# Loading and transposing x ahead of the adaLN product, with the small loads on ScalarE's queue

## The chip, the cores and the metric

The kernel runs on one core of a Trainium2 chip. The metric is the device time of one execution in microseconds; the kernel before takes 868.68 us (median of three executions).

## The reference

One layer of a decoder: 512 tokens, width 1024, float32. Only its beginning matters here:

```python
c_act = silu(c)
mod = c_act @ ada_w + ada_b                 # 1024 -> 6 * 1024
shift1, scale1, gate1, shift2, scale2, gate2 = split(mod, 6)
u = x * (1.0 + scale1) + shift1
q, k, v, lru_x, lru_gate, gate_a, gate_b = split(u @ w_in)   # 1024 -> 5376
y = sigmoid(gate_a) * attention(q, k, v) + sigmoid(gate_b) * rg_lru(lru_x) * gelu(lru_gate)
x = layer_norm(ALPHA * x + gate1 * (y @ w_out))
# then a routed mixture of 16 experts, and a second layer norm
```

So nothing of the large product `u @ w_in` can start before the first third of `mod` (shift1 and scale1, "mod1") is there, which needs 8 MB of `ada_w`, and before x is there.

## The kernel before

Each engine has an instruction stream written out by hand; semaphores order them. Products are taken channel-major: u is held transposed (`uT`, 8 blocks k of 128 channels by 512 tokens), and each weight tile and u are split into a rounded float32r part and the rest (`uh`, `ul`; `whi`, `wlo`), so that a product is three matmuls (L1267 to L1269).

SyncE (SP) issues, in this order: the constants (`cst`, L372, 346 KB, with the identity for transposes), `ccol`, four broadcast pieces of `ada_b` (L375), five small parameter loads (L383), eight 1 MB slices of `ada_w` (`ada1`, L385), four 512 KB pieces of x (L387), and the first three weight tiles of `w_in` (L395; tiles 0, 1, 2, each 512 KB in runs of 512 bytes). Then it stores a small bias table (L405), waits for that store, loads two 512 KB weights of the recurrence (`wax`, L423 and L424) and goes on with the weight tiles from tile 3. Weight tile t waits until the buffer of tile t-3 is split (`split_lo`). Between tiles 5 to 8 it also issues four replications of the bias table, DRAM to DRAM, 768 KB each (L411), and after tile 6 two small copies of k (L433, L434).

GpSimd (POOL) issues at the start twelve small loads, the last of them `rbr` (L511); from the first finished block of `ul` on it loads sixteen further 1 MB slices of `ada_w` (`ada2`, L518) through three buffers, which TensorE frees.

TensorE (PE) works in this order: transpose of the parameters (L1225), the bias table (L1228, which waits for all twelve loads of POOL), the product with `ada1` (`modulate`, L1233, eight steps j, each waiting for its slice), the transpose of its result (L1243), then the 32 transposes of x (L1253) into four PSUM banks, then `project(0)`, `project(1)` and so on, one for each weight tile; the products with `ada2` and the work of the attention and of the recurrence stand between them.

VectorE (DVE) adds the bias (L841), writes shift and scale (L844, L845), then for each pair of blocks computes the odd block of u out of PSUM (L860) and the low parts of both (L856). After the first pair it splits weight tile 0, after the last pair tile 1 (L832); then comes a chain of 24 tiny operations (L870 to L885), and then the split of tile 2. ScalarE (ACT) computes for an even block `uh` and `uT` out of PSUM (L610, L611), for an odd block `uh` out of `uT` (L607), and the high parts of the weight tiles (L589).

Because PE's four banks are refilled only when ACT and DVE have read them, the transposes of the blocks 4 to 7 wait for the blocks 0 to 3.

Of the kernel before, what the change touches and what calls it, by code (L numbers as in the profile page):

```python
# [9 lines left out]
ACT = mybir.ActivationFunctionType  # L10
# [6 lines left out]
P = 128  # L17
D = 1024
KT = D // P
T = 512  # L20
NT = T // P
# [48 lines left out]
C_ID, C_LOW, C_HOT, C_TOK, C_EXP, C_LT, C_GT, C_END = 0, 128, 256, 640, 644, 660, 676, 692  # L70
# [32 lines left out]
def hybrid_layer(nc, x, c, ada_w, ada_b, w_in, attn_sink, rel_bias, conv_w, conv_b, lru_wa, lru_ba,  # L103
# [13 lines left out]
    with ctx:  # L117
# [10 lines left out]
        def at(offset, name, shape, dt=F32):  # L128
            size = 4 * int(np.prod(shape[1:]))
            assert offset + size <= 229344, name  # L130
            return nc.alloc_sbuf_tensor_at(name, shape, dt, offset=offset), offset + size
# [45 lines left out]
        x_sb, _ = at(R_A, "x_sb", [P, NT, D])  # L177
        uT, _ = at(R_B, "uT", [P, KT, T])
        uh, _ = at(R_U, "uh", [P, KT, T], F32R)
# [144 lines left out]
        def sem(name):  # L324
# [16 lines left out]

        names = """setup_done pcol_ps bvec_ps xT_ps u_even u_odd mod1_ps mod1_sb u_hi u_lo split_hi split_lo proj_ps evac
            pcol_sb exp_small dve_order pool_order c_done bvec_sb k_sb conv_done lr_ps li_ps er_done ti_done
# [27 lines left out]
        def _(sp):  # L371
            sp.dma_start(cst[:, :], consts[:, 0:C_END]).then_inc(const_in, 16)  # L372
            sp.dma_start(ccol[:, :], c[0].rearrange("(p j) -> p j", j=8)).then_inc(small_in, 16)
            for g in range(4):
                sp.dma_start(adab1[32 * g:32 * g + 32, :], ada_b[0, g * 512:(g + 1) * 512].partition_broadcast(32))\  # L375
                    .then_inc(adab_in, 16)
            for j, (a, b) in enumerate(((conv_w[0].rearrange("j (k p) -> (j k) p", p=P), 32),
                                        (conv_b[0].rearrange("(k p) -> k p", p=P), 8),
                                        (lru_ba[0].rearrange("(k p) -> k p", p=P), 8),
                                        (lru_bx[0].rearrange("(k p) -> k p", p=P), 8),  # L380
                                        (lru_lambda[0].rearrange("(k p) -> k p", p=P), 8))):
                r = (0, 32, 40, 48, 56)[j]
                sp.dma_start(prm[r:r + b, :], a).then_inc(param_in, 16)  # L383
            for j in range(8):
                sp.dma_start(ada1[:, j, :], ada_v[:, j, 0:2 * D]).then_inc(ada1_sem[j], 16)  # L385
            for t in range(NT):
                sp.dma_start(x_sb[:, t, :], x[0, t * P:(t + 1) * P, :]).then_inc(x_in, 16)  # L387

# [181 lines left out]
        def _(act):  # L570
            A = act.activation

            act.wait_ge(small_in, 16)
            A(tiny[:, 0, :], ccol[:, :], ACT.Exp, scale=-1.0).then_inc(S["exp_small"], 1)
# [4 lines left out]
            act.wait_ge(S["bvec_ps"], 1)  # L579
            A(bvec[:, :], psum[0:16, 6, 0:384], ACT.Copy).then_inc(S["bvec_sb"], 1)  # L580

            def split(t):
# [20 lines left out]
            for k in range(KT):  # L603
                bias_, scale_ = mod1[:, k:k + 1], mod1[:, 8 + k:9 + k]
                if k % 2 == 1:
                    act.wait_ge(S["u_odd"], k // 2 + 1)
                    A(uh[:, k, :], uT[:, k, :], ACT.Copy).then_inc(S["u_hi"], 1)  # L607
                else:
                    act.wait_ge(S["xT_ps"], k + 1)
                    A(uh[:, k, :], bank[XB[k % 4]], ACT.Identity, bias=bias_, scale=scale_).then_inc(S["u_hi"], 1)  # L610
                    A(uT[:, k, :], bank[XB[k % 4]], ACT.Identity, bias=bias_, scale=scale_).then_inc(S["u_even"], 1)  # L611
                if k == 1:
                    split(0)
# [185 lines left out]
        def _(dve):  # L799
# [58 lines left out]
            for k in range(0, KT, 2):  # L858
                dve.wait_ge(S["xT_ps"], k + 2)
                V.tensor_scalar(uT[:, k + 1, :], bank[XB[(k + 1) % 4]], mod1[:, 9 + k:10 + k], mod1[:, k + 1:k + 2],  # L860
                                ALU.mult, ALU.add).then_inc(S["u_odd"], 1)
                u_low(k)
                u_low(k + 1)
                if k == 0:
                    split(0)
# [354 lines left out]
        def _(pe):  # L1220
# [10 lines left out]
            def modulate(j, weights, out_, done):  # L1231
# [3 lines left out]
                ins.then_inc(done, 1)  # L1235

            pe.wait_ge(S["c_done"], 1)
            for j in range(8):
# [5 lines left out]
            ins.then_inc(S["mod1_ps"], 1)  # L1244
            pe.wait_ge(x_in, 16 * NT)
            for k in range(KT):
                if k >= 4:
                    pe.wait_ge(S["u_hi"], k - 3)
                    pe.wait_ge(S["u_even"], (k - 4) // 2 + 1)
                    if k % 2 == 1:  # L1250
                        pe.wait_ge(S["u_odd"], (k - 4) // 2 + 1)
                for t in range(NT):
                    ins = nc.tensor.transpose(bank[XB[k % 4]][:, t * P:(t + 1) * P], x_sb[:, t, k * P:(k + 1) * P], ident)  # L1253
                ins.then_inc(S["xT_ps"], 1)

            def project(s):
# [240 lines left out]
```

## Time and profile before

| | us |
|---|---|
| median of three executions | 868.68 |
| lowest, highest | 868.55, 869.92 |
| the profiled execution | 869.77 |
| its span | 868.1 |

The page of the profile has these two lines among others (busy time and share of the span by engine; the span in 40 slices of 21.7 us, busy share in tenths):

```profile
PE 751.2 (87%) x3605; PEld 588.0 (68%) x3605; DVE 605.0 (70%) x885; ACT 473.9 (55%) x737; POOL 87.5 (10%) x113
PE   3699689999999999999974699999999999999900
DMA  8988586463122222249428699998599999663162
```

PE is busy for 87% of the span; the first six slices, some 130 us, are the part in which it isn't. What matters for a change in the first 45 us is whether a shift there is carried through that part.

### The profile page before, as it was taken

To read this page: it belongs to the slowest core of one execution; us is meant where nothing else is said; L and a number is where in the kernel's file an instruction comes from. 1 tells how busy PE (TensorE), PEld (TensorE's weight loads), DVE (VectorE), ACT (ScalarE), POOL (GpSimd) and SP (SyncE) were. 2 spreads that over 40 slices of the span, in tenths; PEclk is the share of its full clock that TensorE was granted. 3 is DMA by queue.
4 is the path that set the end of the run, shared out by engine and by line. 5 is a ranking of instruction groups with operands and counts; after the bars stand their busy time and mean duration, and the time that the engine had idled before them with its cause. 6 is when DMAs were issued, how large, how long until landed. Compare 5 with 4: busy or idle time off the path is not lost.

```text
span 868.1 us, 11627 instructions
## 1 busy us (share of the span) xinstructions
PE 751.2 (87%) x3605; PEld 588.0 (68%) x3605; DVE 605.0 (70%) x885; ACT 473.9 (55%) x737; POOL 87.5 (10%) x113
## 2 busy tenths in 40 slices
PE   3699689999999999999974699999999999999900
PEld 0375355688877888878863577777777777777700
DVE  0372444396797645666976688898888898988738
ACT  1242234657536555451010678888778888878634
POOL 3000000200000000000660001010001010001030
PEclk9799689999999999999965799999999999999955
DMA  8988586463122222249428699998599999663162
GB/s 312 360 277 299 170 300 230 158 195 98 50 66 80 74 73 73 70 158 372 176 82 322 225 399 394 399 382 316 189 396 383 400 395 386 267 238 150 48 218 97
DMA packets 111232, 201.28 MB, mean 232 GB/s; under 512 B 6248, under 2 KB 55624, under 8 KB 108128
## 3 DMA queue, kind: packets, MB, share of 16 engines
q1 hardware_dynamic: 100736, 155.18, 50.2%
q0 software_dynamic: 10464, 45.69, 14.0%
q8 instruction: 17, 0.28, 0.1%
q14 instruction: 15, 0.12, 0.0%
HBM read 182.20 MB, written 21.54 MB: 235 GB/s over the span
## 4 chain that ended last, share of the span: by engine, by line
PE 65%; DVE 15%; DMA 8%; SPq 6%; ACT 3%; issue 3%; DVEq 0%; POOL 0%; POOLq 0%; ACTq 0%
PE psum L1437 8%; PE psum L1439 8%; PE psum L1438 8%; PE psum L1267 6%; PE psum L1268 6%; PE psum L1269 6%; PE psum L1443 4%; DMA raw<-in_w_in_dram 4%; PE psum L1444 4%; PE psum L1446 4%; DMA x_sb<-in_x_dram 3%; PE psum L1303 3%; SPq L411 2%; PE psum L1331 2%; DVE u L1037 2%
## 5 line engine op out<-in xcount | busy, mean ns | idle before, releaser
L1152 DVE TENSOR_TENSOR mlo<-mraw,mhi 128x1024 fp32r<-128x1024 f32 x198 | 226.9, 1220 | 15.2 <-ACT mhi L728 15.1
L728 ACT ACTIVATE mhi<-mraw 128x1024 fp32r<-128x1024 f32 x216 | 214.8, 1052 | 17.6 <-PE psum L1439 7.6
L1267 PE MATMUL psum<-uh,whi 128*128 128x512 f32 x336 | 139.3, 415 | 0.8 <-DVE wlo L832 0.8
L1268 PE MATMUL psum<-ul,whi 128*128 128x512 f32 x336 | 132.0, 393 | 0.0
L1269 PE MATMUL psum<-uh,wlo 128*128 128x512 f32 x336 | 131.7, 392 | 0.0
L1437 PE MATMUL psum<-mhi,xTh 128*128 128x512 f32 x288 | 112.9, 392 | 4.4 <-DVE mlo L1152 4.4
L832 DVE TENSOR_TENSOR wlo<-raw,whi 128x1024 fp32r<-128x1024 f32 x42 | 51.3, 1223 | 88.1 <-ACT whi L589 88.1
L1438 PE MATMUL psum<-mlo,xTh 128*128 128x512 f32 x288 | 112.7, 391 | 0.0
L1439 PE MATMUL psum<-mhi,xTl 128*128 128x512 f32 x288 | 112.7, 391 | 0.0
L1267 PEld LDWEIGHTS psum<-uh,whi 128*128 128x128 f32 x336 | 63.8, 190 | 22.4 <-issue 7.8
L1268 PEld LDWEIGHTS psum<-ul,whi 128*128 128x128 f32 x336 | 63.8, 190 | 14.4 <-issue 2.5
L1269 PEld LDWEIGHTS psum<-uh,wlo 128*128 128x128 f32 x336 | 63.6, 189 | 13.8
L1437 PEld LDWEIGHTS psum<-mhi,xTh 128*128 128x128 f32 x288 | 54.5, 189 | 16.2 <-DVE mlo L1152 4.8
L1439 PEld LDWEIGHTS psum<-mhi,xTl 128*128 128x128 f32 x288 | 54.5, 189 | 11.4
L1438 PEld LDWEIGHTS psum<-mlo,xTh 128*128 128x128 f32 x288 | 54.5, 189 | 11.3
L589 ACT ACTIVATE whi<-raw 128x1024 fp32r<-128x1024 f32 x42 | 44.1, 1052 | 33.0 <-DMA raw<-in_w_in_dram 33.0
L1443 PE MATMUL psum<-mhi,hTh 128*128 128x512 f32 x144 | 58.1, 403 | 4.4 <-DVE hTl L1178 4.4
L1444 PE MATMUL psum<-mlo,hTh 128*128 128x512 f32 x144 | 56.2, 390 | 0.0
L1446 PE MATMUL psum<-mhi,hTl 128*128 128x512 f32 x144 | 44.4, 389 | 0.0
L698 ACT ACTIVATE ssb<-ssb,negm 128x256 f32<-128x256 f32 (+1 forms) x64 | 30.0, 470 | 23.4 <-DVE sm L930 23.3
L755 ACT ACTIVATE hTh<-psum 128x256 fp32r<-128x256 f32 x36 | 12.8, 384 | 48.7 <-PE psum L1459 48.7
L532 POOL TENSOR_TENSOR x<-row,row 128x1024 f32<-128x1024 f32 x4 | 13.5, 3386 | 254.6 <-DVE row L1029 254.6
(260 smaller groups left out, 1128.2 us busy)
## 6 DMA issues: line engine op xcount, KB each, us to landing
mraw<-in_moe_w_gate_dram SPq DMA_DIRECT2D x64, 512.0 KB, 5.5
mraw<-in_moe_w_up_dram SPq DMA_DIRECT2D x64, 512.0 KB, 7.7
mraw<-in_moe_w_down_dram SPq DMA_DIRECT2D x64, 512.0 KB, 8.3
raw<-in_w_in_dram SPq DMA_DIRECT2D x42, 512.0 KB, 4.0
ada<-in_ada_w_dram POOLq DMA_DIRECT2D x16, 1024.0 KB, 7.4
y_d<-ysb POOLq DMA_DIRECT2D x19, 512.0 KB, 7.0
ada<-in_ada_w_dram SPq DMA_DIRECT2D x8, 1024.0 KB, 13.5
y_d<-zrow POOLq DMA_DIRECT2D x8, 512.0 KB, 6.3
```

The lines of the kernel that those rows point to most:

```text
L728: A(mhi[ch % HLR][:, :, :], mraw[par][ch][:, :].rearrange("p (k f) -> p k f", k=2), ACT.Copy)\
L832: V.tensor_tensor(wlo[t % 3][:, :, :], r3, whi[t % 3][:, :, :].bitcast(F32), ALU.subtract)\
L1152: V.tensor_tensor(mlo[ch % HLR][:, :, :], mraw[par][ch][:, :].rearrange("p (k f) -> p k f", k=2), mhi[ch % HLR][:, :, :].bitcast(F32), ALU ...
L1267: mmul(bank[s % 2], h[:, k, :], uh[:, k, :], start=(k == 0), stop=False)
L1268: mmul(bank[s % 2], h[:, k, :], ul[:, k, :], start=False, stop=False)
L1269: ins = mmul(bank[s % 2], l[:, k, :], uh[:, k, :], start=False, stop=(k == KT - 1))
L1437: mmul(o_, xTh[:, k, :], h[:, i, :], start=first, stop=False)
L1438: mmul(o_, xTh[:, k, :], l[:, i, :], start=False, stop=False)
L1439: ins = mmul(o_, xTl[:, k, :], h[:, i, :], start=False, stop=last)
L1443: mmul(bank[5 + i], hTh[:, k, :], h[:, i, :], start=(k == 0), stop=False)
L1444: mmul(bank[5 + i], hTh[:, k, :], l[:, i, :], start=False, stop=False)
L1446: ins = mmul(bank[5 + i], hTl[:, k, :], h[:, i, :], start=False, stop=(k == FT - 1))
```

## The change

- x is issued first on SP's queue, then `ada1`, then the weight tiles 0 to 2.
- The constants, `ccol`, the parameter loads and the pieces of `ada_b` are issued by ACT at the head of its stream, in this order, ahead of its first instruction.
- PE does the 32 transposes of x ahead of `modulate`. A bank is refilled when ACT has copied it.
- ACT copies each transposed block to a new SBUF tile `xT`, eight copies, before it waits for mod1.
- ACT and DVE then compute the blocks of u out of `xT` and not out of PSUM. `uT` moves to the region of `x_sb`, so DVE first waits for all eight copies.

```diff
-        uT, _ = at(R_B, "uT", [P, KT, T])
+        xT, _ = at(R_B, "xT", [P, KT, T])
+        uT, _ = at(R_A, "uT", [P, KT, T])
@@ sync
-            sp.dma_start(cst[:, :], consts[:, 0:C_END]).then_inc(const_in, 16)
-            sp.dma_start(ccol[:, :], c[0].rearrange("(p j) -> p j", j=8)).then_inc(small_in, 16)
...
+            for t in range(NT):
+                sp.dma_start(x_sb[:, t, :], x[0, t * P:(t + 1) * P, :]).then_inc(x_in, 16)
             for j in range(8):
                 sp.dma_start(ada1[:, j, :], ada_v[:, j, 0:2 * D]).then_inc(ada1_sem[j], 16)
-            for t in range(NT):
-                sp.dma_start(x_sb[:, t, :], x[0, t * P:(t + 1) * P, :]).then_inc(x_in, 16)
@@ scalar
+            act.dma_start(cst[:, :], consts[:, 0:C_END]).then_inc(const_in, 16)
+            act.dma_start(ccol[:, :], c[0].rearrange("(p j) -> p j", j=8)).then_inc(small_in, 16)
+            for j, (a, b) in enumerate(((conv_w[0].rearrange("j (k p) -> (j k) p", p=P), 32),
...
+                act.dma_start(prm[r:r + b, :], a).then_inc(param_in, 16)
+            for g in range(4):
+                act.dma_start(adab1[32 * g:32 * g + 32, :], ada_b[0, g * 512:(g + 1) * 512].partition_broadcast(32))\
+                    .then_inc(adab_in, 16)
...
+            for k in range(KT):
+                act.wait_ge(S["xT_ps"], k + 1)
+                A(xT[:, k, :], bank[XB[k % 4]], ACT.Copy).then_inc(S["xT_sb"], 1)
...
-                    act.wait_ge(S["xT_ps"], k + 1)
-                    A(uh[:, k, :], bank[XB[k % 4]], ACT.Identity, bias=bias_, scale=scale_).then_inc(S["u_hi"], 1)
-                    A(uT[:, k, :], bank[XB[k % 4]], ACT.Identity, bias=bias_, scale=scale_).then_inc(S["u_even"], 1)
+                    act.wait_ge(S["xT_sb"], k + 1)
+                    A(uh[:, k, :], xT[:, k, :], ACT.Identity, bias=bias_, scale=scale_).then_inc(S["u_hi"], 1)
+                    A(uT[:, k, :], xT[:, k, :], ACT.Identity, bias=bias_, scale=scale_).then_inc(S["u_even"], 1)
@@ vector
-                dve.wait_ge(S["xT_ps"], k + 2)
-                V.tensor_scalar(uT[:, k + 1, :], bank[XB[(k + 1) % 4]], mod1[:, 9 + k:10 + k], mod1[:, k + 1:k + 2],
+                dve.wait_ge(S["xT_sb"], KT)
+                V.tensor_scalar(uT[:, k + 1, :], xT[:, k + 1, :], mod1[:, 9 + k:10 + k], mod1[:, k + 1:k + 2],
@@ tensor
+            pe.wait_ge(x_in, 16 * NT)
+            for k in range(KT):
+                if k >= 4:
+                    pe.wait_ge(S["xT_sb"], k - 3)
+                for t in range(NT):
+                    ins = nc.tensor.transpose(bank[XB[k % 4]][:, t * P:(t + 1) * P], x_sb[:, t, k * P:(k + 1) * P], ident)
+                ins.then_inc(S["xT_ps"], 1)
+
             pe.wait_ge(S["c_done"], 1)
             for j in range(8):
                 pe.wait_ge(ada1_sem[j], 16)
...
-            pe.wait_ge(x_in, 16 * NT)
-            for k in range(KT):
-                if k >= 4:
-                    pe.wait_ge(S["u_hi"], k - 3)
-                    pe.wait_ge(S["u_even"], (k - 4) // 2 + 1)
-                    if k % 2 == 1:
-                        pe.wait_ge(S["u_odd"], (k - 4) // 2 + 1)
```

## Rows read from the trace of the kernel before

**Rows 1.** Chain that ended last, 0 to 135 us: start, duration, what.

```profile
12.54 22.06 DMA x_sb<-in_x_dram
...
41.49 14.25 DMA raw<-in_w_in_dram
...
97.66 19.57 DMA raw<-in_w_in_dram
```

**Rows 2.** Timeline of SP's queue: start, duration, engine, line, operation, tiles, count.

```profile
0.86 0.39 SPq L372 DMA_DIRECT2D cst<-in_consts_dram  x1
...
5.50 3.98 SPq L385 DMA_DIRECT2D ada<-in_ada_w_dram  x8
9.52 5.27 SPq L387 DMA_DIRECT2D x_sb<-in_x_dram  x4
14.83 19.56 SPq L395 DMA_DIRECT2D raw<-in_w_in_dram  x3
34.43 1.61 SPq L405 DMA_DIRECT2D bias_vec_d<-bvec  x1
40.02 0.37 SPq L423 DMA_DIRECT2D wax<-in_lru_wa_dram  x1
...
54.88 0.76 SPq L411 DMA_DIRECT2D bias_rep_d<-bias_vec_d  x1
```

**Rows 3.** Windows: length; PE, PEld, DVE, ACT, POOL busy (count); clock, DMA share, GB/s.

```profile
1.00:2.00 1.00, 0.00 (x0) 0.00 (x0) 0.31 (x4) 1.00 (x1) 0.58 (x1) 1.00 0.21 28
1.00:9.00 8.00, 0.33 (x1) 0.18 (x1) 0.50 (x6) 1.57 (x3) 6.63 (x12) 1.00 0.69 219
9.00:34.60 25.60, 12.88 (x70) 2.66 (x70) 1.62 (x7) 0.69 (x2) 0.00 (x0) 0.90 1.02 401
34.60:39.00 4.40, 4.36 (x21) 4.36 (x22) 2.10 (x3) 2.88 (x4) 0.57 (x2) 0.50 1.20 290
39.00:40.00 1.00, 0.85 (x5) 0.61 (x3) 0.82 (x1) 1.00 (x3) 1.00 (x2) 0.73 0.85 157
40.00:42.00 2.00, 0.79 (x5) 0.58 (x6) 1.90 (x4) 1.32 (x3) 0.04 (x1) 1.00 0.85 279
42.00:55.00 13.00, 12.21 (x54) 9.54 (x54) 11.33 (x35) 6.80 (x10) 0.00 (x0) 1.00 1.06 349
90.00:94.00 4.00, 0.00 (x0) 0.00 (x0) 0.00 (x0) 0.60 (x1) 0.00 (x0) 0.50 0.25 99
120.00:160.00 40.00, 40.00 (x169) 24.66 (x168) 18.80 (x26) 15.95 (x24) 2.11 (x4) 0.94 0.63 202
```

**Rows 4.** Timeline of PE, DVE and ACT; in brackets the idle time before.

```profile
14.36 1.43 PE L1228 MATMUL psum<-cst,rbs 33*16 33x384 f32 x2 [5.88 <-DMA rbr_sb<-in_router_b_dram]
...
26.98 1.06 PE L1233 MATMUL psum<-ada,cact 128*32 128x512 f32 x8 [1.42 <-DMA ada<-in_ada_w_dram]
29.48 1.93 PE L1233 MATMUL psum<-ada,cact 128*32 128x512 f32 x8 [1.43 <-DMA ada<-in_ada_w_dram]
...
32.33 1.11 PE L1243 MATMUL psum<-cst,mod1row 128*128 128x128 f32 x4 [0.92 <-DVE mod1row L841]
...
33.56 0.16 DVE L845 TENSOR_SCALAR mod<-psum 128x8 f32<-128x8 f32 x1
...
35.86 0.78 ACT L610 ACTIVATE uh<-psum,mod 128x512 fp32r<-128x512 f32 x1 [19.56 <-PE psum L1253]
36.72 0.81 DVE L860 TENSOR_SCALAR uT<-psum,mod 128x512 f32<-128x512 f32 x1 [3.01 <-PE psum L1253]
...
45.34 1.41 DVE L856 TENSOR_TENSOR ul<-uT,uh 128x512 fp32r<-128x512 f32 x2
...
53.22 1.23 DVE L832 TENSOR_TENSOR wlo<-raw,whi 128x1024 fp32r<-128x1024 f32 x1
63.02 0.54 DVE L945 TENSOR_SCALAR xc<-xpad,pcol 128x512 f32<-128x512 f32 x1
```

**Rows 5.** Source line L395, 54 to 56 us (weight tile 5): its time to landing.

```profile
DMA to landing us min/median/max: 4.4/4.4/4.4
```

More of the change, by code:

```diff
@@ L340, in hybrid_layer @@
         fgather = [sem(f"fgather{i}") for i in range(NT)]
-        names = """setup_done pcol_ps bvec_ps xT_ps u_even u_odd mod1_ps mod1_sb u_hi u_lo split_hi split_lo proj_ps evac
+        names = """setup_done pcol_ps bvec_ps xT_ps xT_sb u_even u_odd mod1_ps mod1_sb u_hi u_lo split_hi split_lo proj_ps evac
             pcol_sb exp_small dve_order pool_order c_done bvec_sb k_sb conv_done lr_ps li_ps er_done ti_done
@@ L371, in _ @@
         def _(sp):
-            sp.dma_start(cst[:, :], consts[:, 0:C_END]).then_inc(const_in, 16)
-            sp.dma_start(ccol[:, :], c[0].rearrange("(p j) -> p j", j=8)).then_inc(small_in, 16)
[L374 to L383, printed above, removed]
+            for t in range(NT):
+                sp.dma_start(x_sb[:, t, :], x[0, t * P:(t + 1) * P, :]).then_inc(x_in, 16)
             for j in range(8):
                 sp.dma_start(ada1[:, j, :], ada_v[:, j, 0:2 * D]).then_inc(ada1_sem[j], 16)
-            for t in range(NT):
-                sp.dma_start(x_sb[:, t, :], x[0, t * P:(t + 1) * P, :]).then_inc(x_in, 16)
             def load_tile(t):
@@ L571, in _ @@
             A = act.activation
+            act.dma_start(cst[:, :], consts[:, 0:C_END]).then_inc(const_in, 16)
+            act.dma_start(ccol[:, :], c[0].rearrange("(p j) -> p j", j=8)).then_inc(small_in, 16)
+            for j, (a, b) in enumerate(((conv_w[0].rearrange("j (k p) -> (j k) p", p=P), 32),
+                                        (conv_b[0].rearrange("(k p) -> k p", p=P), 8),
+                                        (lru_ba[0].rearrange("(k p) -> k p", p=P), 8),
+                                        (lru_bx[0].rearrange("(k p) -> k p", p=P), 8),
+                                        (lru_lambda[0].rearrange("(k p) -> k p", p=P), 8))):
+                r = (0, 32, 40, 48, 56)[j]
+                act.dma_start(prm[r:r + b, :], a).then_inc(param_in, 16)
+            for g in range(4):
+                act.dma_start(adab1[32 * g:32 * g + 32, :], ada_b[0, g * 512:(g + 1) * 512].partition_broadcast(32))\
+                    .then_inc(adab_in, 16)
             act.wait_ge(small_in, 16)
@@ L1244, in _ @@
             ins.then_inc(S["mod1_ps"], 1)
-            pe.wait_ge(x_in, 16 * NT)
-            for k in range(KT):
-                if k >= 4:
-                    pe.wait_ge(S["u_hi"], k - 3)
-                    pe.wait_ge(S["u_even"], (k - 4) // 2 + 1)
-                    if k % 2 == 1:
-                        pe.wait_ge(S["u_odd"], (k - 4) // 2 + 1)
-                for t in range(NT):
-                    ins = nc.tensor.transpose(bank[XB[k % 4]][:, t * P:(t + 1) * P], x_sb[:, t, k * P:(k + 1) * P], ident)
-                ins.then_inc(S["xT_ps"], 1)
             def project(s):
```

## The prediction

> **What bounds the kernel now.** I read the chain that ended last first, because it says whether the first 45 us matter at all. They do. Its early links are one after the other the landing of x (12.54 to 34.60), a short stretch of transposes and of ACT and DVE work, the landing of weight tile 3 (issued 41.49, landed 55.74), SP's queue, and the landing of tile 9 (97.66 to 117.23) [rows 1]. From 120 us on PE is busy without a gap [rows 3]; what is gained or lost by then stays to the end.
>
> The windows say what kind of bound it is. From 9.0 to 34.6 us the DMA share is 1.02, from 34.6 to 39 it is 1.20, from 42 to 55 it is 1.06 [rows 3]: the transfers, not their issue, fill the time. Gaps are in two places: 1 to 9 us has a share of 0.69, and 40 to 42 has 0.85 [rows 3]. Later the bound narrows: in 90 to 94 us the share is 0.25 at 99 GB/s while PE does nothing [rows 3]. That is a quarter of the 16 DMA engines. I read it as the bias replications, whose outer dimension is 4, holding four engines; the weight tiles in the same queue have to pass those four. The four replications begin at 54.88 [rows 2], just behind tile 5, which was issued at 54.47 and took 4.4 us to land [rows 5]. So the first 58.9 us are measured by when tile 5 has landed and the replications get their turn.
>
> **The small loads.** SP begins with the constants at 0.86 and comes to the first large load at 5.50 [rows 2]: 4.6 us of issuing. After the change x goes out at 0.86. But issue isn't the limit. In 1 to 9 us the DMA engines are empty for (1 - 0.69) x 8 = 2.5 us; in the second from 1 to 2 a queue that has just started is empty for 0.79 us in any case, and a tenth more may go in the next [rows 3]. 2.5 - 0.9 = 1.6 us come back. The bytes ahead of weight tile 0 are the same, so all of x and ada1 has landed at 34.6 - 1.6 = 33.0. Bounds: no gain (34.6), if small packets that now meet the large ones hold them up as much as the gap did, and 2.4 us (32.2). I take 1.6, since the share behind it is 1.02 already.
>
> The Trainium skill (DMA: Bandwidth & Descriptors, "Issuing engines are not separate DMA queues") says that starting DMAs from several engines saves only the time that the sequencer takes to issue them. Taken as the whole saving that would be 4.6 us; the trace's share of 0.69 and 1.02 allows only 1.6 of it.
>
> ACT now issues 11 loads of about 0.4 us, 4.6 us in all, ahead of its first instruction, and its early results come up to some 5 us later than the 4 us of now. Cover: nobody needs them before the first modulate, and PE's bias table waits for POOL's last load until 14.36 [rows 4]. Without that cover it would cost those microseconds.
>
> **x first, ada1 last.** Now ada1 is complete at 29.4, mod1 at 33.72, and x lands only at 34.60, so the wait for mod1 is hidden behind x [rows 1, 4]. After the change ada1 lands last, at 33.0, and the whole tail stands bare behind it. The tail of today, 29.48 to 33.72, is 4.25 us: 1.93 for the last modulate, the addition, 1.11 for four transposes, two small DVE operations [rows 4]. It ran at the half clock. At full clock the slice before it took 1.06 [rows 4] and the four transposes would take about 0.6: 2.9 us. mod1 is there at 33.0 + 4.25 = 37.25, or at 35.9. PE has the same sparse pattern of one slice each 2.5 us ahead of it as today, when the clock fell before the last slice, so I take 37.25. Today it is 33.72: mod1 comes 3.5 us later.
>
> **The transposes.** They can't start when x lands, since in PE's stream they stand behind the bias table (14.36 + 1.43 = 15.8) [rows 4]. 32 of them and eight copies of about 0.6 us end near 22; by then three or four slices wait, 0.86 us each, and PE has caught up near 25, 8 us ahead of the last slice. So they are hidden, and POOL's loads could be 8 us later before it cost anything. What they leave: today ACT's first block starts at 35.86, 2.1 us after mod1, DVE's at 36.72 [rows 4]; after, both start within 0.1 us of mod1, at 37.3.
>
> **The blocks of u.** Today DVE goes from 36.72 to 46.75, 10.0 us [rows 4]. After: the odd block comes out of SBUF, for which the nearest row is the 0.54 us of L945 against 0.81 out of PSUM [rows 4]. That saves 3 x 0.2; the first pair costs 0.7 more, because DVE now starts with ACT and not behind it. Again 10.0 us. The low parts are complete at 37.3 + 10.0 = 47.2 instead of 46.75 (or at 45.9 with the fast tail). Behind it stand the split of tile 1, the tiny chain and the split of tile 2, which ends at 54.45 today [rows 4] and at 54.9 after (or 53.7). So the 2.1 us of transposes removed behind mod1, the 0.9 us wait for x and the shorter landing just pay for the late mod1.
>
> **PE's clock.** The granted clock was 0.50 while PE did nothing but transposes from 34.6 on, 0.73 in 39 to 40, and 1.00 from 40 [rows 3]: the transposes brought the full level (2.4 GHz) back before project(0). After the change PE is idle between mod1 and the first split weight tile (about 41.4), and starts project(0) at the half level. 24 matmuls at 0.43 us instead of 0.23 for the first 5 us: it ends near 49.6 instead of 47.8, project(1) near 55.3. Tile 2's split comes at 54.9, so PE is 0.4 to 0.9 us late at 55. Cover: PE waits with nothing to do around 90 to 94 us [rows 3]. Without that it would cost 0.9.
>
> The Trainium skill (TensorE: Matmul & The Clock Gate, "Part 4: PE-mode transpose") says that transposes don't count as activity for the clock. By that rule moving them away could cost no clock, and project(0) would be no slower than today. The trace speaks against it: the clock rose amid nothing but transposes.
>
> **The queue up to tile 5.** The weight tiles 0 to 2 follow ada1 and are done at 39.9 - 1.6 = 38.3; the store of the bias table, which waits behind them from 34.43 to 40.0 [rows 2], is back 1.6 us earlier, so wax goes out at 38.4. Its first bytes come 1.3 us later; POOL's first three ada2 loads go out when the first low part is there, at 39.4 against 38.4. So the DMA engines stand empty for about 1.4 us around 39, where today the stretch 39 to 42 lost 0.15 + 2 x 0.15 = 0.45 us [rows 3]. Of the 1.6 us some 0.9 are lost again: 0.7 us of gain up to the landing of tile 5, 58.9 - 0.7 = 58.2. Tile 5 is issued at 54.9, and the backlog reaches over that. With the fast tail the issue is earlier but the backlog the same: again 0.7. Bounds: 1.6 (no new gap) and, where the issue of tile 5 decides, the loss below.
>
> **Sum.** From the replications on SP isn't gated by compute, and the queue hands 0.7 us on to tile 9 and to PE: 868.1 - 0.7 = 867.4 us of span. The profiled execution took 869.77, 1.1 above the median; on the median, 868.68 - 0.7 = 868.0 us. 0.2% (1.7 us) is about what a measurement of this kernel can tell from no change.
>
> **The rivals.**
> - *The bare tail decides (slower).* The landing gains nothing and the tail runs at the half clock: mod1 at 34.6 + 4.25 = 38.85, low parts at 48.85, tile 2 split and tile 5 issued 2.1 us later than now, and with it the replications. It decides once the low parts end later than about 48.0, where tile 5's issue passes the backlog. 868.68 + 2.1 = 870.8. For it: ada1 has nothing behind which to hide, and the time that the small packets cost is unknown. Against it: the gap in 1 to 9 us is plain.
> - *All the early gap comes back (faster).* 2.4 us of landing and a fast tail: mod1 at 35.1, ada2 1.9 us earlier than in my sum, so no new gap at 39, and 2.0 us go through the queue. 866.7. For it: the transfers are the bound all the way. Against it: the clock, and a queue that starts from nothing.
> - *The change doesn't do what it says.* The transposes wait for POOL's loads, which under x and ada1 come 8 us or more later, and run into the last slices; or the later queue takes up any shift. Then nothing or little is moved: 868.7.
>
> **How the numbers follow.** The forecast 0.50, slower 0.18, faster 0.24, no effect 0.08. Same is 0.58. The range takes in both outer cases with their bounds, 865.8 to 871.0.
>
> **What would show it.** x's transposes from about 16 to 22; last slice landed at 33.0; L845 at 37; L610 right behind; last L856 ending near 47; wax issued near 38.4; tile 5 landed near 58.2; PE at full clock only some 5 us into project(0); project(8), now at 122.78, 0.7 earlier. Wrong if the last slice lands after 34, if SP is blocked elsewhere between 58 and 117, or if the replications don't follow tile 5.

## The result, and the profile after

| | median us | span of the profiled execution |
|---|---|---|
| before (same chip, six executions) | 869.65 | 868.1 |
| changed | 872.71 | 872.8 |

The ratio is 1.0039, interval 1.0025 to 1.0053: the change makes the kernel 3 us slower. The forecast was 868.0, 0.7 us faster. The profiled execution of the changed kernel took 874.81 and is the longest of its six; the spans of the other five are 869.9 to 871.3. Its 4.7 us against the span of before are therefore the upper end of what the change costs; what follows looks for where they arise, and takes the price from the medians.

The timeline of PE, ACT and DVE after, to be held against [rows 4] (start, duration, engine, line; in brackets the idle time before):

```profile
19.92 5.52 PE L1246 MATMUL psum<-cst,x_sb 128*128 128x128 f32 x32
...
36.86 1.93 PE L1237 MATMUL psum<-ada,cact 128*32 128x512 f32 x8 [0.64 <-DMA ada<-in_ada_w_dram]
...
40.94 0.15 DVE L849 TENSOR_SCALAR mod<-psum 128x8 f32<-128x8 f32 x1
41.13 0.81 ACT L614 ACTIVATE uh<-xT,mod 128x512 fp32r<-128x512 f32 x1 [14.90 <-DVE mod L849]
...
45.43 0.80 PE L1268 MATMUL psum<-uh,whi 128*128 128x512 f32 x1 [4.61 <-DVE wlo L836]
...
57.59 2.36 DVE L836 TENSOR_TENSOR wlo<-raw,whi 128x1024 fp32r<-128x1024 f32 x2
59.03 0.40 PE L1268 MATMUL psum<-uh,whi 128*128 128x512 f32 x1
```

The transposes (L1246) are over at 25.4 and nobody waits for them. The last slice of ada1 is used at 36.86 (in the kernel before the last slice at 29.48, and x, the later of the two, at 34.6 [rows 1, 4]). The tail follows bare, mod1 is there at 41.1 instead of 33.7, and the first block of u begins 5.3 us later than in [rows 4]. The split of tile 2 starts at 57.59 instead of 53.22.

SP's queue after, to be held against [rows 2]:

```profile
0.86 2.24 SPq L374 DMA_DIRECT2D x_sb<-in_x_dram  x4
3.14 6.53 SPq L376 DMA_DIRECT2D ada<-in_ada_w_dram  x8
...
36.65 1.67 SPq L394 DMA_DIRECT2D bias_vec_d<-bvec  x1
41.97 0.38 SPq L412 DMA_DIRECT2D wax<-in_lru_wa_dram  x1
...
59.25 0.79 SPq L400 DMA_DIRECT2D bias_rep_d<-bias_vec_d  x1
```

SP's large loads start 4.6 us earlier, and yet everything that SP issues behind weight tiles 0 to 2 is later: the store of the bias table by 2.2, wax by 2.0, the first replication by 4.4 us (54.88 before).

The windows, to be held against [rows 3] (length; busy time of PE, PEld, DVE, ACT, POOL; clock, DMA share, GB/s):

```profile
1.00:9.00 8.00, 0.00 (x0) 0.00 (x0) 0.31 (x4) 1.28 (x1) 6.63 (x12) 1.00 0.84 228
9.00:34.60 25.60, 13.23 (x87) 7.05 (x91) 0.88 (x5) 5.51 (x12) 0.00 (x0) 0.99 1.02 380
40.00:45.00 5.00, 0.82 (x4) 0.41 (x2) 2.93 (x6) 3.87 (x6) 1.26 (x3) 0.50 0.42 121
```

Two things stand in them. The share in 1 to 9 us rose from 0.69 to 0.84, but the bytes only from 219 to 228 GB/s, and from 9 to 34.6 the same share of 1.02 moves 380 GB/s instead of 401: the DMA engines are busy for longer with the same bytes. And in 40 to 45 us they stand idle for more than half of the time, where the kernel before had this row:

```profile
40.00:45.00 5.00, 3.79 (x20) 3.12 (x21) 4.89 (x8) 4.18 (x7) 0.04 (x1) 1.00 0.95 363
```

The chain that ended last, to be held against [rows 1]:

```profile
7.94 28.88 DMA ada<-in_ada_w_dram
...
102.33 19.32 DMA raw<-in_w_in_dram
...
127.20 0.43 PE psum L1268
```

Instead of x, ada1 is now its first long link, and it ends 2.2 us later, at 36.8. From there on the distance to the kernel before grows to 4.4 us at the first replication and then stays nearly the same: tile 9 is issued at 102.33 (97.66 before), and project(8) starts at 127.20 (122.78 before).

### The profile page after: what moved, and what is told of

It reads as the page before. It is cut to its first block, busy times and chain, and to the rows that moved or that the text cites. A ratio compares the mean times of both kernels' runs of the same rounds, so it can differ in the third digit from the quotient of the medians.

```text
span 872.8 us, 11631 instructions
## 1 busy us (share of the span) xinstructions
PE 751.9 (86%) x3605; PEld 589.3 (68%) x3605; DVE 603.5 (69%) x885; ACT 478.4 (55%) x745; POOL 87.7 (10%) x113
## 3 DMA queue, kind: packets, MB, share of 16 engines
q1 hardware_dynamic: 100144, 154.53, 49.9%
## 4 chain that ended last, share of the span: by engine, by line
PE 66%; DVE 15%; DMA 7%; SPq 5%; ACT 3%; issue 3%; DVEq 0%; POOL 0%; POOLq 0%; ACTq 0%
PE psum L1438 8%; PE psum L1440 8%; PE psum L1439 8%; PE psum L1268 7%; PE psum L1270 7%; PE psum L1269 7%; PE psum L1444 4%; PE psum L1445 4%; PE psum L1447 4%; DMA ada<-in_ada_w_dram 3%; PE psum L1304 3%; DMA raw<-in_w_in_dram 2%; SPq L400 2%; SPq L422 2%; PE psum L1332 2%
## 5 line engine op out<-in xcount | busy, mean ns | idle before, releaser
L836 DVE TENSOR_TENSOR wlo<-raw,whi 128x1024 fp32r<-128x1024 f32 x42 | 51.2, 1222 | 88.2 <-ACT whi L593 88.0
```

The costliest lines, as they stand in the source:

```text
L836: V.tensor_tensor(wlo[t % 3][:, :, :], r3, whi[t % 3][:, :, :].bitcast(F32), ALU.subtract)\
```

## The experiments

All ratios are held against the kernel before in the same series, whose median was 869.65 to 870.22. Each kernel has 4 to 12 executions, and most intervals are about 0.1 to 0.2% to each side, so 1 us is hardly told apart from nothing. The last three columns are us from the start of one profiled execution.

| kernel | median us | ratio to before, interval | x and ada1 landed | mod1 | first replication issued |
|---|---|---|---|---|---|
| before | 868.68 to 870.22 | 1 | 34.6 | 33.7 | 54.9 |
| changed | 872.71 | 1.0039 (1.0025 to 1.0053) | 36.8 | 41.1 | 59.3 |
| smalls_act | 872.89 | 1.0031 (1.0019 to 1.0042) | 37.2 | 35.3 | 57.5 |
| smalls_sp | 873.03 | 1.0030 (1.0019 to 1.0041) | 35.8 | 39.2 | 57.4 |
| before_late | 869.58 | 0.9988 (0.9975 to 1.0000) | 32.9 | 31.1 | 53.6 |
| order_alone | 873.44 | 1.0034 (1.0021 to 1.0047) | 34.6 | 38.2 | 56.4 |
| after_late | 872.58 | 1.0026 (1.0014 to 1.0037) | 33.4 | 37.7 | 55.9 |
| after_gate | 873.13 | 1.0033 (1.0021 to 1.0046) | 36.9 | 40.3 | 58.5 |
| after_late_gate | 869.78 | 0.9997 (0.9988 to 1.0006) | 33.1 | 36.0 | 54.2 |
| after_warm | 873.81 | 1.0047 (1.0033 to 1.0062) | | 40.8 | 58.9 |
| before_late_gate | 872.03 | 1.0021 (1.0012 to 1.0030) | 32.9 | 31.5 | 57.3 |
| before_spread | 852.89 | 0.9798 (0.9780 to 0.9816) | 35.1 | 33.4 | 55.4 |
| after_spread | 857.71 | 0.9858 (0.9844 to 0.9873) | 36.2 | 39.6 | 57.8 |
| before_sl | 851.29 | 0.9784 (0.9766 to 0.9802) | 33.0 | 32.1 | 55.2 |
| before_slt | 849.23 | 0.9789 (0.9754 to 0.9825) | 32.8 | 31.9 | 53.4 |
| after_slt | 853.75 | 0.9808 (0.9795 to 0.9821) | 33.2 | 37.4 | 53.1 |
| before_sltg | 858.68 | 0.9876 (0.9861 to 0.9891) | 33.2 | 32.0 | 55.0 |

"Landed" is the start of the PE work that waited for the later of the two. In after_warm the added matmuls stand between the slices and hide it.

**The two halves of the change.** smalls_act is the kernel before with only the small loads moved to ACT:

```diff
-            sp.dma_start(cst[:, :], consts[:, 0:C_END]).then_inc(const_in, 16)
...
+            act.dma_start(cst[:, :], consts[:, 0:C_END]).then_inc(const_in, 16)
```

> The kernel before with the small loads issued by ACT; x stays behind ada1, transposes stay behind mod1. Theory (small loads beside the large ones slow these down): x lands at about 36.8 instead of 34.6 although the first slice of ada1 is issued 4.6 us earlier, and the kernel is some 2 us slower than before. Rival (order alone): x lands at 33 to 34.6 and the kernel is as fast as before or up to 1.6 us faster.

smalls_sp is the changed kernel with them back at the head of SP's queue.

> The changed kernel with the small loads back at the head of SP's queue, ahead of x; everything else as changed. Theory: two causes add up. One is that the small loads on ACT's queue run beside x and ada1 and make those slower (last ada1 slice landed at 36.8 where the kernel before had everything landed at 34.6); the other is that the tail behind ada1 (4.2 us) stands bare. Then the last slice lands near 34.6 here, mod1 comes near 38.9 instead of 41.1, and the kernel is some 2 us faster than the changed one, still 2 us slower than before. Rival (the queue of the small loads is innocent, order alone does it): last slice at 36.8 again and the time of the changed kernel.

Each half alone costs nearly what both cost together. In smalls_act ada1 is issued first, at 0.86, and x must have landed before PE can transpose; timeline of PE and windows of smalls_act:

```profile
37.24 4.70 PE L1253 MATMUL psum<-cst,x_sb 128*128 128x128 f32 x24 [2.23 <-DMA x_sb<-in_x_dram]
```

```profile
1.00:9.00 8.00, 0.00 (x0) 0.00 (x0) 0.31 (x4) 1.28 (x1) 6.63 (x12) 1.00 0.89 248
9.00:34.60 25.60, 12.24 (x71) 3.13 (x71) 1.57 (x6) 1.12 (x4) 0.00 (x0) 0.99 1.02 363
```

A share of 0.89 and 1.02, near the 0.84 and 1.02 of the changed kernel, and only 248 and 363 GB/s: x lands 2.6 us later than in the kernel before, although the order of the large loads is the same and the first of them starts 4.6 us earlier. The theory holds, its rival (order alone) falls. The records of the single packets in the traces say where the time goes. Each column is the time that packets took until the last one of x and ada1, in us of all 16 DMA engines together; "idle" is what is left of the time from the start of the span. The moved loads are those that the change gives to ACT. PE starts on the data some 0.6 us after the time in the first column, which is what the table above calls landed.

```
              last of     x    ada1   moved   POOL's   tile 0   rest   idle
              x, ada1                 loads   loads    ahead
before          34.0     5.2   21.3    2.0     1.8      0.3     0.4    3.0
smalls_act      36.6     5.2   23.7    2.1     3.3      0.9     0.3    1.1
changed         36.3     6.2   21.2    2.5     3.1      1.4     0.3    1.6
smalls_sp       35.2     6.5   20.0    2.2     2.0      1.2     0.4    2.9
order_alone     34.0     5.8   20.0    2.1     0.1      1.8     0.4    3.8
before_late     32.3     5.2   20.5    2.1     0.1      0.3     0.4    3.7
```

In smalls_act 1.9 us of idle time come back, but the same packets take 4.5 us more: those of ada1 2.4, POOL's 1.5 and weight tile 0's 0.6 (of tile 0 more packets run ahead of the last one of x). The moved loads themselves take no longer than at the head of SP's queue; it is ada1 and POOL's loads, which now run beside them, that do. In the changed kernel 1.4 us of idle time come back, and x takes 1.0 us more, POOL's loads 1.3, the moved loads 0.5, and 1.1 us of tile 0 run ahead. Whether the mixing of three queues or the broadcast reads of `ada_b` is what makes packets slow was not tried.

smalls_sp landed at 35.8, not at the 34.6 of its theory: without ACT's queue 1.0 us of the loss is gone. The other 1.2 us belong to the order: x's packets take 1.3 us more at the head of the queue, and 0.9 us more of tile 0 run ahead of ada1's last packet, while ada1's take 1.3 us less. mod1 came at 39.2 (38.9 expected), and the kernel is not measurably faster than the changed one, where some 2 us were expected.

Each half moves the first replication by 2.6 and 2.5 us in the traces, both together by 4.4, which is nearly the sum. The medians don't add up like that: 2.7 and 2.8 us for the halves, 3.1 for both. The longest of six executions is the one in the changed kernel's trace; whether this is all of the difference no run shows.

**Order alone.** before_late and after_late issue ten of POOL's twelve small loads behind its third ada2 load; order_alone is after_late with the small loads of ACT back at the head of SP's queue, so nothing small runs beside x. It differs from before_late by the order of x and ada1 and by the copies.

```diff
             pool.wait_ge(S["u_lo"], 1)
             for n in range(NA2):
...
+                if n == A2_BUFS - 1:
+                    for h in range(2):
+                        for g in range(4):
+                            lo_ = 2 * D + (4 * h + g) * 512
+                            pool.dma_start(adab2[32 * g:32 * g + 32, h, :], ada_b[0, lo_:lo_ + 512].partition_broadcast(32))\
+                                .then_inc(S["pool_late"], 16)
...
-            pe.wait_ge(S["pool_in"], 16 * 12)
+            pe.wait_ge(S["pool_in"], 16 * 2)
```

> The kernel before with the same ten loads of POOL moved behind its third ada2 load. Theory: x lands near 33 instead of 34.6, and up to 1.5 us of it reach the end (the loads come back in the full stretch of 42 to 55, so 0.8 faster is my number). Rival (the start of the replications is set by the total of bytes alone): no change.

> x and its transposes ahead of ada1 as in the changed kernel, but the small loads at the head of SP's queue and ten of POOL's twelve behind its third ada2 load, so that nothing small runs beside x. It differs from the run before_late in the order alone. Theory (the bare tail is a cost of its own): x and ada1 have landed near 33 in both; here the tail of 3 to 4.2 us follows, mod1 comes at 36 to 37.3 and the u chain starts there, against 35.0 in before_late (x landed 32.9, ACT's first block 2.1 later), and the kernel is 1 to 2 us slower than before_late (869.6). Rival (all of the loss was the small packets): no difference to before_late.

Timeline of PE and ACT in before_late:

```profile
32.89 5.38 PE L1254 MATMUL psum<-cst,x_sb 128*128 128x128 f32 x24 [2.07 <-DMA x_sb<-in_x_dram]
34.11 0.78 ACT L610 ACTIVATE uh<-psum,mod 128x512 fp32r<-128x512 f32 x1 [24.69 <-PE psum L1254]
```

Timeline of PE, DVE and ACT in order_alone:

```profile
14.70 5.75 PE L1247 MATMUL psum<-cst,x_sb 128*128 128x128 f32 x32 [6.05 <-DMA x_sb<-in_x_dram]
...
34.59 1.73 PE L1238 MATMUL psum<-ada,cact 128*32 128x512 f32 x8 [0.60 <-DMA ada<-in_ada_w_dram]
...
38.02 0.16 DVE L849 TENSOR_SCALAR mod<-psum 128x8 f32<-128x8 f32 x1
38.21 0.81 ACT L614 ACTIVATE uh<-xT,mod 128x512 fp32r<-128x512 f32 x1 [16.97 <-DVE mod L849]
```

The order is a cost of its own, and a larger one than its theory said: 873.44 against 869.58 for before_late, 3.9 us instead of 1 to 2. The first block of u starts 4.1 us later (38.21 against 34.11). Of this 2.4 us are the tail: 3.6 us from the last slice to the first block of u, against 1.2 us from x's landing to it in before_late. The theory had 2.1 there and so put ACT's first block in before_late at 35.0, which is 0.9 us too late. The other 1.7 us are the landing, 34.6 and not 32.9. The packets of x and ada1 together take as long in both (25.8 and 25.7 us in the table above); what differs is that 1.8 us of tile 0's packets run before ada1's last one, against 0.3 us before x's last one.

before_late landed 1.7 us earlier than before, as expected, and is 0.6 us faster by its median, with an interval that reaches to nothing. That raised the question where 1.7 us can go.

**Which limit holds the replications.** after_late is the changed kernel with the edit above; after_gate is the changed kernel with one line:

```diff
-            pool.wait_ge(S["u_lo"], 1)
+            pool.wait_ge(S["mod1_ps"], 8)
```

> The changed kernel, but ten of POOL's twelve small loads (adab2, router weights and bias) are issued only behind its third ada2 load. Theory (packets of three queues side by side are what costs): the last ada1 slice lands at 33 to 34 instead of 36.8, the bias table's product no longer waits until 18.5, and the kernel is 2 to 3 us faster than the changed one, near the time of before. Rival (the ada1 product is late for a cause other than these loads, or the transfer only moves into the full stretch behind mod1): the landing moves by no more than the 1.5 us that their 0.6 MB need, and the time by less than 1 us.

> The changed kernel, but POOL issues its first three ada2 loads when the last modulate of ada1 is done (38.8) and not when the first low part of u is (43.7). Theory: what the late mod1 costs is time of the DMA engines; they stand idle for some 3 us between 40 and 45, because ada2, wax and tile 3 all wait for things behind mod1. Filled earlier, the share of 40 to 45 goes from 0.42 to about 0.9 and the kernel is 2 us faster than the changed one. Rival (the chain on ACT and DVE decides: mod1, u, the split of tile 2, the issue of tile 5 and the replications, at 59.25): tile 5 and the replications are issued when they are now, and the time doesn't move by more than 0.5 us.

Both do in the trace most of what they should, and neither changes the time measurably. Timeline of DVE and ACT in after_late (the second row is the split of tile 3, which had been awaited), and the time to landing of its tile 5, issued at 55.5:

```profile
37.51 0.16 DVE L849 TENSOR_SCALAR mod<-psum 128x8 f32<-128x8 f32 x1
...
57.42 1.06 ACT L593 ACTIVATE whi<-raw 128x1024 fp32r<-128x1024 f32 x1 [5.72 <-DMA raw<-in_w_in_dram]
```

```profile
DMA to landing us min/median/max: 5.3/5.3/5.3
```

mod1 came 3.4 us earlier than in the changed kernel, tile 5 was issued 3.3 us earlier, but tile 3 landed no earlier than there (57.25). The stretch in which the DMA engines stand idle is still there, only earlier:

```profile
38.00:42.00 4.00, 0.00 (x0) 0.00 (x1) 2.82 (x5) 4.00 (x6) 1.69 (x4) 0.50 0.42 122
```

And the ten loads that were taken out of the first 15 us are issued from 41.9 on, beside tile 3. Windows and SP's queue of after_gate:

```profile
40.00:45.00 5.00, 0.39 (x1) 0.39 (x2) 3.75 (x8) 4.39 (x6) 0.00 (x0) 0.50 1.07 410
```

```profile
58.47 0.79 SPq L400 DMA_DIRECT2D bias_rep_d<-bias_vec_d  x1
```

Here the idle stretch of the DMA engines is gone (1.07 instead of 0.42), and the first replication is still issued only at 58.5, since DVE's chain ends only 0.8 us earlier than it did. This made a new theory, with a prediction that the old ones don't share.

> The edits of after_late and of after_gate together in the changed kernel. Each alone gave nothing: after_late made mod1 3.5 us earlier, but tiles 3 and 4 landed when they did (57.4, 59.2); after_gate filled the gap of the DMA engines between 40 and 45, but tile 5 was issued only 0.8 us earlier. Theory (the replications start at the later of two times, the issue of tile 5 behind VectorE's chain and the landing of the tiles queued before it, and in the changed kernel both are at 59 to 60): together they move both, tile 4 lands at 57 or earlier with tile 5 issued at 55.9, and the kernel is 2 us or more faster than the changed one (+0.3% over before becomes +0.1% or less). Rival (another limit, unknown): again 872 to 873.

Windows and SP's queue of after_late_gate, and the landing of its tile 5, issued at 53.8:

```profile
40.00:45.00 5.00, 4.64 (x11) 3.67 (x12) 4.39 (x9) 4.66 (x8) 1.75 (x3) 0.50 1.02 408
```

```profile
54.22 0.79 SPq L400 DMA_DIRECT2D bias_rep_d<-bias_vec_d  x1
```

```profile
DMA to landing us min/median/max: 4.1/4.1/4.1
```

Tile 5 landed at 57.9 (60.8 in after_late, 61.9 in after_gate, 62.6 in the changed kernel, 58.9 before), and the time is 869.78, 2.9 us below the changed kernel and equal to before, while its theory allowed up to +0.1% and each edit alone left +0.3%. The start of the replications has two limits, and in the changed kernel both had moved: DVE's chain up to the issue of tile 5, through the late mod1, and the transfers queued ahead of it, through the idle stretch that the late mod1 leaves.

Its counterpart without the changed order is before_late_gate.

> The same two edits in the kernel before. Theory: its chain ends 1.7 us earlier as in before_late, and the DMA engines hardly stand idle in it, so the landing of the tiles is set by bytes: 0 to 1.7 us faster than before, and the distance to after_late_gate is the bare tail of 2 to 4 us. Rival: no distance between the two.

Neither came true. It is slower than before, 872.03 (ratio 1.0021, interval 1.0012 to 1.0030). SP's queue tells why:

```profile
32.72 1.61 SPq L405 DMA_DIRECT2D bias_vec_d<-bvec  x1
49.96 0.37 SPq L423 DMA_DIRECT2D wax<-in_lru_wa_dram  x1
```

POOL's three loads now go out at 29.9, beside x and the weight tiles 1 and 2, and the store of the bias table, which waits behind those, is complete only at 49.9. In the kernel before hardly a gap was there to be filled (a share of 0.95 in 40 to 45). What an earlier start is worth depends on which transfers it comes in front of.

**TensorE's clock.** after_warm adds matmuls that nobody reads to the changed kernel:

```diff
                 modulate(j, ada1[:, j, :], bank[4], S["mod1_ps"])
+                if j >= 2:
+                    mmul(bank[0], ident, x_sb[:, 0, 0:512], start=True, stop=True)
...
             ins.then_inc(S["mod1_ps"], 1)
+            for _ in range(4):
+                mmul(bank[6], ident, cst[:, 128:640], start=True, stop=True)
```

> The changed kernel with idle-time matmuls on TensorE that nobody reads: one behind each modulate from the third on, four behind the transposes of mod1. Theory: half of TensorE's clock costs 1.3 us in the tail behind ada1 and makes project(0) 2 us slower; with the full clock granted from 30 to 51 us mod1 comes at 39.8 instead of 41.1, the split of tile 2 1.3 earlier, and the kernel is about 1.3 us faster than the changed one. Rival (DMA decides up to 120 us): no change in time although mod1 comes earlier.

The full clock was granted without a break from 30 to 55 us, where the changed kernel had 0.50 from 34 to 51, and project(0) ran at it. But the added matmuls delayed the product with the last slice by 1.0 us, mod1 came only 0.3 us earlier (40.8), and the time is 873.81, no better. So this run alone doesn't tell what a full clock is worth. That the slower project(0) costs next to nothing is seen in the changed kernel itself: project(2) starts at 59.03, 0.2 us behind the end of the split of tile 2, which it has to wait for in any case. What a faster tail alone would give isn't shown. In after_gate, whose first 36 us are those of the changed kernel, the last slice happened to run at the full clock and mod1 came 0.8 us earlier, without a gain that the times show.

**The replications themselves.** before_spread and after_spread exchange the two outer dimensions:

```diff
-                src = bass.AP(bias_vec_d.tensor, 4 * hg * 384, [[384, 4], [0, P], [1, 384]])
-                sp.dma_start(bias_rep_d[4 * hg:4 * hg + 4], src).then_inc(bias_dma, 16)
+                src = bass.AP(bias_vec_d.tensor, 4 * hg * 384, [[0, P], [384, 4], [1, 384]])
+                sp.dma_start(bias_rep_d[4 * hg:4 * hg + 4].rearrange("h p n -> p h n"), src).then_inc(bias_dma, 16)
```

> The kernel before with the bias replications' outer dimension the 128 rows and not the 4 heads. Theory (the four engines that hold the replications are what blocks SP and the weight tiles from 55 to 117): the stretches with a DMA share of 0.25 vanish, tile 7 lands some 10 us earlier than 93.4, PE's waits of 10.1 and 3.4 us go, and the kernel is 10 to 13 us faster. Rival (a replication is slow for another cause, its reads or its small packets): under 3 us.

> The changed kernel with the same replications over 128 rows. Theory: PE is then the bound from project(2) on, and project(2) starts 4.4 us later than in the kernel before, so the changed kernel stays 3 to 4.4 us behind the other one of this pair. Rival (the queue of the replications alone carried the loss through): with the replications out of the way the two are within 1 us of each other.

SP's queue of before_spread, and its windows:

```profile
57.58 1.04 SPq L411 DMA_DIRECT2D bias_rep_d<-bias_vec_d  x1
58.73 1.35 SPq L433 DMA_DIRECT2D kk<-kk  x1
```

```profile
58.00:75.00 17.00, 17.00 (x88) 11.80 (x87) 9.09 (x11) 3.69 (x5) 1.58 (x3) 1.00 1.05 378
90.00:94.00 4.00, 4.00 (x26) 2.59 (x28) 3.02 (x5) 0.60 (x1) 0.00 (x0) 1.00 1.06 356
```

The small copy that blocked SP for 12.66 us takes 1.35, the stretches at a share of 0.25 are gone [rows 3], PE has no gap left between 56 and 200 us, and the kernel is 17 us faster, more than the 10 to 13 expected. With the replications out of the way the changed order still costs 4.8 us (857.71 against 852.89). PE is busy without a gap from project(2) to 200 us in both, so it is PE, not the queue, that now carries the late start through. In the traces project(2) starts 2.4 us later (57.4 against 55.0, where 4.4 were expected) and the spans differ by 2.4 us too; why the medians differ by twice that isn't shown. The rival of after_spread is refuted.

Two further edits make the fastest version: ten of POOL's small loads late, as above (with the replications over 128 rows this is before_sl), and DVE's chain of tiny operations (25 of the 26 that the trace has between the two splits) done while it waits for the bias of ada1 (before_slt).

> The kernel before with the replications over 128 rows and ten of POOL's small loads behind its third ada2 load. In before_late the 1.7 us of earlier landing were gone again by tile 9. Theory: with the replications out of the way PE is the bound from 55 us on, and what project(2) starts earlier stays: up to 1.7 us faster than before_spread (852.9). Rival (the ten loads merely return in the full stretch of 42 to 55): the time of before_spread.

> As before_sl, and the chain of 23 tiny operations on VectorE (5.0 us, between the splits of tiles 1 and 2) done while VectorE waits for the bias of ada1. Theory: the split of tile 2 ends 5 us earlier, but TensorE is still in project(1), so project(2) gains only the 0.7 us that it waits today; 0.5 to 1 us faster than before_sl. Rival (tile 5 and all that queues behind it come up to 5 us earlier and this counts): 2 us or more.

> The changed kernel with all three edits of before_slt. Theory: POOL's packets are gone, ACT's remain beside x (as in after_late: landed 33.4, mod1 37.6), and the tail is bare: 2 to 4 us slower than before_slt. Rival (the change pays once its side effects are mended): as fast or faster.

before_slt takes 849.23, by its ratio 2.1% less than before (its interval is wide, 0.9754 to 0.9825, since two of its six executions took 856.33 and 857.49 and the other four 848.38 to 849.77). before_sl takes 851.29, ratio 0.9784 with 0.9766 to 0.9802; the two can't be told apart, and before_sl is not measurably faster than before_spread. The median of after_slt is 4.5 us behind that of before_slt, though the intervals overlap because of those two executions; nothing speaks for the rival that the changed order pays once its side effects are mended.

> before_slt with POOL's first three ada2 loads issued when the last modulate of ada1 is done. Theory: TensorE is the bound from 45 us on, in before_slt it stands still only for about 2 us between 42 and 60; at most 1 us faster than before_slt (849.2). Rival: the ada2 loads now come in front of the weight tiles and delay project(3): slower by up to 2 us.

It takes 858.68, 9.5 us more than before_slt: the rival's mechanism, the one seen in before_late_gate, with four times its price. wax is issued at 49.23 instead of 38.47, and the split of tile 1 waits until 47.2 for the tile. project(1) starts at 49.6 instead of 46.5, and at the half clock, and project(2) at 58.0 instead of 52.1. From there to 200 us PE has no gap in which the delay could be absorbed. This is 5.9 of the 9.5 us; where the rest arises wasn't looked for.

## Why the prediction was wrong

**The small loads (the first step that failed).** It put the landing of x and ada1 at 33.0, with 34.6 as the upper bound; it was 36.8. The gap in the DMA engines' first microseconds was real, and as much of it came back as was forecast: 1.4 us of idle time, where the sum had 1.6. But the step took a gap in busy time for a gap in bytes. It put at nothing what packets cost that now run side by side and in another order. In the changed kernel x's took 1.0 us more, POOL's small loads 1.3, the moved ones 0.5, and 1.1 us of weight tile 0 ran ahead of ada1's last packet. The bound "no gain" was not a bound: smalls_act shows the move of the small loads alone making x land 2.6 us later than before. The term, forecast as -1.6, measured +2.2; smalls_sp, with the small loads back on SP's queue, still has +1.2 of it, which is the part of the order.

What stands in the Trainium skill (DMA: Bandwidth & Descriptors, "Issuing engines are not separate DMA queues"), that DMAs from several engines run on the same 16 DMA engines and interleave, agrees with this trace. The same section of the Trainium skill says that starting them from several engines saves only issue time. The issue time was saved, 4.6 us of it, and the transfers still ended 2.2 us later.

**The bare tail (right in mechanism).** 4.25 us were forecast at the half clock, and 36.86 to 41.09 is 4.2. The idle time between mod1 and the first block of u was gone, as forecast, and the blocks of u took 10.1 us where 10.0 were forecast. With the landing as measured these steps give the last low part complete at 36.8 + 4.25 + 10.0 = 51.1; it was 51.2.

**The transposes and the clock (right).** They ran from 19.9 to 25.4 instead of 16 to 22, because the bias table waited until 18.5 for POOL's loads, and were hidden all the same. project(0) began at the half clock, with a matmul each 0.43 us for its first 5.3 us, and project(2) was no more than 0.2 us later for it.

**The queue (the second step that failed).** The prediction let a backlog of transfers hold the replications, put the idle time that a late mod1 leaves at 1.4 us, and gave 0.7 us of gain. The landing alone doesn't explain the miss: in after_late x and ada1 landed at 33.4 and mod1 came at 37.7, within 0.5 us of the forecast 33.0 and 37.25, and the kernel is still 2.4 us slower than before and not 0.7 faster. The backlog was there, but the idle time was near 3 us in the changed kernel (40 to 45) and 2.3 in after_late (38 to 42). One part of it the prediction didn't have: the first packet of POOL's ada2 loads comes 2.9 us after their issue in the changed kernel (43.7 to 46.7) and 1.3 us after it in the kernel before; why, no run shows. Both limits of the replications then lay at 59 to 60 us, and tile 5 landed at 62.6 in place of the forecast 58.2. after_late, after_gate and after_late_gate show that neither edit alone brings the time back and both together do, to the time of before but not below it. after_late also has ten loads beside tile 3 that the prediction's sum hasn't, so how its 2.4 us divide is open.

**The rival.** "The bare tail decides" was the case that came, with its chance of 0.18. It priced the loss at 2.1 us for a landing of 34.6; with the measured 36.8 its own sum gives 2.1 + 2.2 = 4.3, and the first replication was issued 4.4 us later, tile 9 was split 4.4 us later, and the profiled span was 4.7 us longer. The medians differ by 3.1 only. Part of this is that the profiled execution is the longest of its six; the rest I can't place.

## What to carry to other kernels

A free stretch in the DMA engines' busy share is not free bandwidth: small loads beside large ones made the large ones' packets take longer here, so ask what they cost where they are going, not only what they cost where they are. When two inputs are needed, load last the one with the shorter way to its first use; here x's transposes (1.2 us to the first block) behind ada1's tail of 4.2 us were the better order. And a queue that issues in order has two limits, the issue and the backlog: moving one of them alone showed nothing here.

## What the runs showed of the hardware

- A DRAM to DRAM replication of 768 KB whose outer dimension is 4 ran at 99 GB/s with a DMA share of 0.25, and a small copy behind it blocked SP for 12.7 us; with the outer dimension 128 the kernel is 17 us faster. The Trainium skill (DMA: Bandwidth & Descriptors, "Why a DMA increments its semaphore by 16 and not by 1") says that a DMA is split over the largest number of engines up to 16 that divides the slowest dimension of both its sides. That is four for the one form and sixteen for the other, and the share agrees: 0.25 is four of sixteen, and with the other form it is 1.05 in 58 to 75 us.
- x's packets of 4 KB took 163 ns on average behind ada1 and more at the head of the queue in every run: 193 ns beside two other queues (changed), 204 ns beside one (smalls_sp), 181 ns with the other queues nearly empty (order_alone). So the other queues are not needed to make them slow. Moving ten small loads out of the first 15 us brought the landing of 10 MB forward by 1.7 us in one kernel and 3.4 us in the other, for 0.6 MB moved.
- A short store in a queue behind 1.5 MB of weight tiles completes with them, 5.6 us after its issue in the kernel before and 17 us in before_late_gate; whoever waits for it on that queue waits for all of that.
